# Stick-breaking attention: the last head pair's gate product placed inside its first two steps, and the first output tile computed row by row around the last value products

## The reference, cut to what matters

```python
def stick_breaking_attention(q, k, v):          # 16 heads of 64, 528 tokens in blocks of 128
    ...
    for i in range(nb):
        kend = (i + 1) * BLOCK
        z = jnp.einsum('bqhd,bkhd->bhqk', qp[:, i * BLOCK:kend], kp[:, :kend]) * scale
        valid = (kpos >= META_PAD) & (kpos < qpos)
        log_beta = jax.nn.log_sigmoid(z)
        log_1m = jnp.where(valid, jax.nn.log_sigmoid(-z), 0.0)
        after = lax.cumsum(log_1m, axis=3, reverse=True) - log_1m
        a = jnp.where(valid, jnp.exp(log_beta + after), 0.0)
        outs.append(jnp.einsum('bhqk,bkhd->bqhd', a, vp[:, :kend]))

def stick_breaking_mixer(h, w_in, w_out):
    q, k, v, g = _split(h @ w_in, SB_SPLITS)
    o = stick_breaking_attention(q.reshape(shp), k.reshape(shp), v.reshape(shp))
    return (o.reshape(b, l, SB_WIDTH) * jax.nn.silu(g)) @ w_out
```

## Time and profile before

| what | value |
|---|---|
| median of 3 runs | 2283.48 us (2282.42 to 2287.58) |
| profiled execution, its own time | 2283.47 us |
| its span in the trace | 2281.7 us |
| mean granted TensorE clock in it | 0.965 of full speed |

### The profile page before, as it was taken

One profiled execution on the slowest core, in us unless ns is written; L12 is line 12 of the kernel. 1 busy time (PEld: TensorE's weight loads), 2 busy tenths in 40 slices (PEclk: granted clock), 3 DMA queues, 4 the chain that ended last, 5 costly groups with the idle time before them and its releaser, 6 DMA issues.

```text
span 2281.7 us, 33033 instructions
## 1 busy us (share of the span) xinstructions
PE 2140.4 (94%) x13426; PEld 1833.3 (80%) x13426; DVE 1219.0 (53%) x1594; ACT 783.6 (34%) x1267; POOL 675.1 (30%) x314
## 2 busy tenths in 40 slices
PE   4999989999999997999999999999999896999987
PEld 3888878888888885889777888888898685988866
DVE  3886868544565546560963322223789325066752
ACT  2312232221122224332873333223333633255542
POOL 0322323222222222222993444444030223300002
PEclk9999999999999999999999999999998897999998
DMA  7443315233243311221322333333222011221210
GB/s 291 132 146 131 130 39 183 84 96 109 98 147 101 117 60 50 71 61 51 46 51 75 107 91 97 92 92 95 72 84 65 10 51 33 84 64 58 56 47 37
DMA packets 74953, 199.92 MB, mean 88 GB/s; under 512 B 25296, under 2 KB 26576, under 8 KB 74832
## 3 DMA queue, kind: packets, MB, share of 16 engines
q1 hardware_dynamic: 73648, 197.60, 28.3%
q10 hardware_dynamic: 1184, 0.61, 0.1%
HBM read 194.51 MB, written 2.10 MB: 86 GB/s over the span
## 4 chain that ended last, share of the span: by engine, by line
PE 85%; DVE 6%; POOL 3%; issue 2%; ACT 2%; DMA 1%; SPq 0%; DVEq 0%; ACTq 0%
PE ps L2044 60%; PE ps L2159 5%; PE ps L2516 5%; PE ps L2059 4%; POOL NAP L856 2%; PE ps L2565 1%; PE ps L2069 1%; DVE ada_acc L1386 1%; PE ps L2540 1%; PE ps L2552 1%; PE ps L2083 1%; PE ps L2220 1%; DVE S L1454 1%; DVE UC L1751 1%; PE ps L2076 1%
## 5 line engine op out<-in xcount | busy, mean ns | idle before, releaser
L809 POOL TENSOR_TENSOR WL<-raw,WH 128x1024 fp32r<-128x1024 f32 x215 | 523.5, 2438 | 1313.7 <-ACT WH L906 1313.5
L906 ACT ACTIVATE WH<-raw 128x1024 fp32r<-128x1024 f32 x260 | 273.9, 1057 | 486.4 <-PE ps L2044 458.9
L2044 PE MATMUL ps<-HH,WH 128*128 128x512 f32 (+2 forms) x1568 | 423.4, 336 | 2.5 <-DVE HL L1853 2.5
L2044 PE MATMUL ps<-HH,WL 128*128 128x512 f32 (+2 forms) x1568 | 418.5, 333 | 0.0
L2044 PE MATMUL ps<-HL,WH 128*128 128x512 f32 (+2 forms) x1568 | 417.8, 333 | 0.0
L2044 PEld LDWEIGHTS ps<-HH,WH 128*128 128x128 f32 x1568 | 251.8, 188 | 37.3 <-issue 3.2
L2044 PEld LDWEIGHTS ps<-HL,WH 128*128 128x128 f32 x1568 | 251.3, 188 | 34.0 <-issue 1.4
L2044 PEld LDWEIGHTS ps<-HH,WL 128*128 128x128 f32 x1568 | 251.2, 188 | 31.1
L2044 PE MATMUL ps<-GH,WH 128*128 128x512 f32 (+1 forms) x896 | 265.5, 354 | 3.0 <-issue 3.0
L2044 PE MATMUL ps<-GH,WL 128*128 128x512 f32 (+1 forms) x896 | 266.3, 355 | 0.0
L2044 PE MATMUL ps<-GL,WH 128*128 128x512 f32 (+1 forms) x896 | 265.1, 353 | 0.0
(11 more groups left out here) (269 smaller groups left out, 3379.1 us busy)
## 6 DMA issues: line engine op xcount, KB each, us to landing
raw<-stream SPq DMA_DIRECT2D x260, 512.0 KB, 3.6
ring<-stream SPq DMA_DIRECT2D x80, 512.0 KB, 3.8
ADA<-stream SPq DMA_DIRECT2D x4, 2048.0 KB, 20.8
XT<-rpb SPq DMA_DIRECT2D x128, 24.0 KB, 2.3
XT<-xT SPq DMA_DIRECT2D x1, 2048.0 KB, 8.6
out<-XT SPq DMA_DIRECT2D x8, 256.0 KB, 2.0
V1s<-V SPq DMA_DIRECT2D x6, 256.0 KB, 4.6
XT<-ctxT SPq DMA_DIRECT2D x1, 1024.0 KB, 11.1
```

The costliest lines, as they stand in the source:

```text
L809: nc.gpsimd.tensor_tensor(WL[:, slot, :], raw[:, slot, :], WH[:, slot, :].bitcast(F32), ALU.subtract).then_inc(lo_done[slot], 1)
L906: nc.scalar.activation(WH[:, slot, :], raw[:, slot, :], ACT.Copy).then_inc(hi_done[slot], 1)
L2044: ins = nc.tensor.matmul(pair(g)[:, cols], lhs, x[:, k, cols], start=first, stop=last)
```

## The change

The last pair's gate product (24 matmuls) moves from step 31 to steps 28 and 29, in three pieces: row blocks 0 and 1 at the end of iteration 28, blocks 2 and 3 between the two turns of iteration 29, and blocks 4 to 7 at the end of iteration 29. Iteration 31 has none. Its way through ScalarE (the sigmoid) and VectorE moves from iteration 32 to the end of iteration 31; in its place ScalarE's upper part of output tile 2 moves to iteration 32, and VectorE's lower part of that tile moves behind the whole loop. TensorE's loop ends one iteration earlier: after the last turns it begins output tile 0 at once, each row block behind a wait for its own part of `o_ready`, with the value products of step 31 set between row blocks 2 and 3. `post(1)` then goes on with output tile 1. The whole diff:

```diff
--- before.py
+++ after.py
@@ -490,6 +490,7 @@
 
         CONV_STEPS = [step for part in CONV_PLAN for step in part]
         NS, NU, NB = len(NA_UNITS), len(SW_UNITS), len(SB_STEPS)
+        LAST_PAIR, LAST_GATE = NB // 2 - 4, NB // 2 - 1
         SB_LOWER = range(TILE["q4", 1] + 3, TILE["g4", KT_D - 1] + 4)
         SW_FULL = [2, 2, 2, 1, 0]
         PT_SB = NS
@@ -1336,7 +1337,7 @@
                     ahead(TILE["q4" if kind == "q" else "k4", m + 1])
 
             for j in range(NB // 2 + 3):
-                if 1 <= j <= NB // 2:
+                if 1 <= j < NB // 2:
                     sb_side(j - 1)
                 if j < NB // 2:
                     sb_sig(2 * j)
@@ -1344,8 +1345,10 @@
                 if 1 <= j <= NB // 2:
                     sb_pt(2 * j - 2)
                     sb_pt(2 * j - 1)
-                if j < NB // 2:
-                    sb_ahead(j)
+                if j == LAST_GATE:
+                    sb_side(LAST_GATE)
+                elif j <= NB // 2:
+                    sb_ahead(min(j, LAST_GATE))
                 if j >= 5 and j % 4 == 1:
                     sb_out(j // 4 - 1)
             post(1)
@@ -2006,7 +2009,11 @@
                     sb_gate(j // 4 - 1)
                 if j < NB // 2:
                     sb_weights(2 * j + 1)
+                if j == LAST_GATE:
+                    sb_side(LAST_GATE)
+                elif j < NB // 2:
                     sb_lower(j)
+            sb_lower(LAST_GATE)
             post(1)
 
 
@@ -2485,7 +2492,7 @@
 
             def post(layer):
                 n, kind, h = ((N2, "out3", H4), (NX, "out4", (OH5, OL5)))[layer]
-                for m in range(KT_D):
+                for m in range(layer, KT_D):
                     project(GROUP[kind, m], TILE[kind, m], h, n)
                 pe.wait_ge(y_sq_used, 7 * layer + 7)
                 token_rstd(GROUP["postc", layer], GROUP["post", layer], n, post_rstd, layer + 1)
@@ -2567,17 +2574,30 @@
                             ins.then_inc(o_full, 1)
 
             all_empty(GROUP["out4", 0])
-            for j in range(NB // 2 + 2):
+            def out_row(k):
+                if k == 3:
+                    sb_pv(NB // 2 - 1)
+                pe.wait_ge(o_ready, KT_D + k + 1)
+
+            for j in range(NB // 2 + 1):
                 if j < NB // 2:
                     sb_s(j)
                 if j >= 2:
                     sb_pv(j - 2)
                 if 1 <= j <= NB // 2:
                     sb_t(2 * j - 2)
+                    if j == LAST_PAIR + 1:
+                        sb_side(LAST_GATE, range(2, 4))
                     sb_t(2 * j - 1)
-                if j < NB // 2:
+                if j < LAST_PAIR:
                     sb_side(j, range(KT_D))
-            pe.wait_ge(o_ready, KT_D + KT_D)
+                elif j == LAST_PAIR:
+                    sb_side(LAST_GATE, range(0, 2))
+                elif j == LAST_PAIR + 1:
+                    sb_side(LAST_GATE, range(4, KT_D))
+                elif j == NB // 2:
+                    pe.wait_ge(sb_om, NB)
+                    project(GROUP["out4", 0], TILE["out4", 0], (OH5, OL5), NX, ready=out_row)
             post(1)
 
 
```

## The result

| | before | after |
|---|---|---|
| median of 5 runs of each | 2285.16 us | 2272.73 us |
| lowest and highest | 2282.42, 2287.67 | 2271.60, 2276.22 |
| span of the profiled execution | 2281.7 us | 2271.7 us |
| its own time | 2283.47 us | 2273.46 us |

The ratio of the times is 0.9947 with a 95% interval of 0.9933 to 0.9962: faster by 12.1 us, between 8.7 and 15.3. The forecast was 11.3 us less and 2272.2 us, with a range of 2270.0 to 2276.4.

What follows compares the result with a forecast made beforehand. TensorE, busy 94% of the span, bounds the kernel through idle and half-clock time in the last pair. Idle removed 6.7 plus half clock removed 4.6 gives 11.3 us: 2283.5 to 2272.2 us, range 2270.0 to 2276.4.

Steps and rivals of the forecast that it cites:

- The idle time: TensorE's six waits in the last pair, 7.9 us: all but 1.2 us would be filled, 6.7 us removed.
- The two waits left: TensorE idle ahead of the value products of steps 29 and 30: 0.4 and 0.8 us, together 1.2.
- the walk: Steps 28 to 30: gate pieces of 6, 6 and 12 matmuls fill waits of 4.77 us with 5.6 us of gate.
- the pieces only delay: Rival, steps 28 to 30: TensorE's lateness passes to VectorE's chain, 1.4 us plus 1.6 of low clock, 2275.2 us; chance 0.06.
- The chain of 2.93 us: Step 31's value products through VectorE, ScalarE and VectorE to the first output matmul; would end at 2212.7.
- the slack of 0.6: Output tile 0: row block 7 finds the last pair's lower part ready 0.6 us before it is needed.
- The waits between row blocks: Output tile 0: eight waits put between matmuls, already met, would cost nothing.
- The clock: Half-clock work behind the 2.58 and 2.28 us waits, 3.23 and 6.07 us, would run at full clock: 4.6 us won.
- the tail: The part behind the output tiles was taken as the same; more clock there, up to 1 us, entered the range's low end.
- the new thin stretch: About 2203.3 to 2207.7: TensorE has 3.2 us of work in 4.4 us, 72%; no clock fall expected, with doubt.
- the two rivals that rest on such a fall: Clock falls at about 2204 to 2207, 2273.8 to 2275.2 us, 0.16; or stays low in output tiles, 0.03 and 0.02.
- The row waits: Rival, output tile 0: row waits hold TensorE as the one wait did, 2.28 us idle, 2277.5 us; chance 0.05.

Runs made afterwards that it cites:

- part 1 alone: Against the kernel before: last pair's gate dealt over steps 28 and 29, output tile 0 still waiting for the whole last pair; ratio 0.9973, stretch 73.81 us.

## Why the prediction was right

**The idle time.** Forecast: 6.7 us of 7.9 go. Measured: 6.9, from 7.93 to 1.00. The two waits left were put at 0.4 and 0.8 us and are 0.30 and 0.68, at the value products that were named. The 0.30 is the one that stood there before.

**The deal.** Step by step the after-trace follows the walk, shifted by 0.92 us since the stretch begins that much later: scores of step 29 forecast for 2193.1, at 2194.20 - 0.92 = 2193.3; scores of step 30 for 2200.0, at 2200.05; row block 0 for 2207.7, at 2207.7. The pieces lie under VectorE's chain and do not push it: VectorE's last mask begins 20.43 us into the stretch against 20.41 before. The two kernels that are not dealt do push it, by 2.5 and 2.2 us, and lose 3.4 and 2.4. The rival "the pieces only delay" describes those two and not the change.

**Tile 0.** The chain of 2.93 us held (2.81 from the start of the value products to the end of `OL5`), and so did the slack of 0.6. Moving the value products by three row blocks later or earlier costs 1.7 and 0.9 us, where 1.6 and 0.6 were expected. The waits between row blocks were costed at nothing. They are nearly that. With the value products ahead of row block 0, the 192 output matmuls stand in one row, with one of the eight waits ahead of them and seven among them:

```profile
2211.13 45.01 PE ps L2051 x192
```

In the kernel with added work, where one wait stands ahead of all, the same 192 took 44.84 us. The difference, 0.17 us, is the most that the eight waits can have cost.

**The clock.** Forecast: 4.6 us. Measured in the two profiles compared: 4.5. Here the agreement owes something to luck. Both figures use the same profile of the kernel before, in which TensorE worked for 6.07 us at half clock behind the last wait; in two others of the same kernel it was 3.4, and the term is then 1.6 + 1.7 = 3.3 and the whole gain in the stretch 10.2. The prediction took this length for fixed, and should have given it as a range of 3 to 6 us. Its own range was wide enough to hold the difference. (The upper end of that range is 2276.2 by its terms, 2275.2 and 1 us of spread, not 2276.4; nothing hangs on it.)

**The rest of the run.** The median fell by 12.4 us and the ratio says 12.1, with an interval from 8.7 to 15.3; the stretch accounts for 10.2 to 11.4. The rest is not shown to be anything but spread, of which there is some in front of the stretch and behind it.

In front of it, the place where the stretch begins moved between 2183.85 and 2191.83 us over the profiles, ahead of all that was changed, and between two profiles of one and the same kernel (part 1 alone) by 6.7 us. Up to there TensorE was busy for 2064.05 us in the first profile of the kernel before and for 2074.35 in the second of part 1 alone, with the same 13033 matmul records:

```profile
0.00:2183.85 2183.85, 2064.05 (x13033) 0.97 0.29 90
```

```profile
0.00:2191.83 2191.83, 2074.35 (x13033) 0.97 0.29 90
```

The same work takes longer. The clock is enough to account for it: summed over slices of 2 us, TensorE had the low clock for 133 us in the first of these and for 150 in the second, and worked in about 92 and 110 of them. By estimate, 18 us more of work at half clock cost 9 us; the beginning of the stretch moved by 8.0. The largest difference stands between 1800 and 2000 us (first the kernel before, then part 1 alone):

```profile
1800.00:2000.00 200.00, 167.34 (x1339) 0.88 0.16 48
```

```profile
1800.00:2000.00 200.00, 171.01 (x1296) 0.84 0.15 45
```

Behind it, the prediction took the tail to stay the same. In the two profiles compared it took 16.9 us before (2281.7 - 2264.78) and 17.4 after (2271.7 - 2254.27). This too is clock, in the 16 matmuls of the tail: 3.43 us before, 3.94 after, and 2.21 in the second profile of the kernel before, whose tail took 15.7 us. First after, then that profile:

```profile
2256.31 1.88 PE ps L2083 x8
2258.83 2.06 PE ps L2090 x8
```

```profile
2267.97 1.07 PE ps L2076 x8
2269.68 1.14 PE ps L2083 x8
```

Over all profiles the tail took 15.7 to 17.4 us, and the stretch therefore compares two kernels better than the whole span does. The two profiled executions differ by 10.0 us: 11.4 in the stretch, less 0.9 in front of it and 0.5 behind it.

**The rivals.** The clock did not fall in the new thin stretch (1.00 from 2184.77 to 2254.25), so neither of the two rivals that rest on such a fall came about. The row waits did not hold TensorE: no wait stands ahead of row block 7. The Trainium skill's rule that was weighed, that recent activity releases the clock (TensorE: Matmul & The Clock Gate, "What's actually happening"), agrees with the run with added work: with throwaway matmuls in the waits the clock was 1.00 throughout.

## What to carry to other kernels

When the last round of a loop whose stages overlap has no filler of its own, look for work that is already due in it and deal it over the waits in pieces that fit: with the gate in one place the whole change took 7 to 9 us off the stretch here, with the deal 10 to 11. The consumer of the last result can start on the parts that are ready, with the producer set inside it far enough ahead to cover its chain; its length can be read off the old trace as the time from the producer's first matmul to the consumer's. Count an idle gap on TensorE together with the half-speed work behind it, and count that as a range, since it differs from run to run.

## What the runs showed of the hardware

- Behind a wait of 2.3 us TensorE worked at half clock for 6.07 us in one profile and for 3.4 us in two others of the same kernel. Waits of 2.6 us ahead of step 30 came with low clock in all four profiles that had them (3.2 to 3.4 us of work in it), and a wait of 1.70 us in the one that had it (3.4 us). Right behind waits of 1.38, 1.1 and 1.05 us the clock was 1.00 in every profile.
- Of ten such low stretches nine lasted 3.4 us and one 6.8, and they began between 0.7 us before and 1.3 us after the end of the wait.
- The place where an unchanged stage begins moved by 8.0 us between profiles, with 133 and 150 us of low clock in front of it.
- Adding 34 useless matmuls to the waits made the kernel 3.4 us faster (ratio 0.9985, 0.9976 to 0.9994).
- Semaphore waits between matmuls that are already met cost next to nothing: at most 0.17 us for eight of them in 192 matmuls (45.01 against 44.84 us).
